# Two halves of one weight, side by side or apart: the order of weight pieces in an expert layer

## The reference

```
logits = t @ router_w                       # 256 tokens, 8 experts
top_v, top_i = top_k(logits, 2)
gates = softmax(top_v)
for e in range(8):
    out += combine[:, e] * ((silu(t @ w1[e]) * (t @ w3[e])) @ w2[e])
```

## Time and profile before

| | us |
|---|---|
| median of 3 runs | 2096.67 |
| lowest and highest run | 2094.08 and 2107.45 |
| the profiled execution's own time | 2105.79 |
| its span | 2104.0 |
| PE busy | 1988.3 (94%) |
| DVE busy | 1509.0 (72%) |
| ACT busy | 1087.0 (52%) |

### The profile page before, as it was taken

How to read it: one execution, slowest core, us unless ns; L and a number is a source line. 1 busy time by engine, 2 the same in 40 slices (tenths; PEclk the granted TensorE clock), 3 DMA queues, 4 the chain that set the end, 5 groups by cost and what they waited for, 6 DMA issues and landing times.

```text
span 2104.0 us, 25252 instructions
## 1 busy us (share of the span) xinstructions
PE 1988.3 (94%) x9922; PEld 1575.0 (75%) x9922; DVE 1509.0 (72%) x1829; ACT 1087.0 (52%) x1148; POOL 85.9 (4%) x78
## 2 busy tenths in 40 slices
PE   8989999999999899998999999999999999999997
PEld 7568588876587588786777777787777775759997
DVE  4666644447575698887789888898989886546666
ACT  1233234322241376775677766777777762535544
POOL 0130000000300000000100000000000000000000
PEclk9999999999999899999999999999999999899999
DMA  8200274343000499897799989999999983226450
GB/s 337 80 1 22 107 292 169 131 160 147 1 1 1 169 426 373 317 383 292 266 360 371 371 321 353 328 377 383 368 353 361 338 314 132 88 100 234 161 200 21
DMA packets 65152, 484.31 MB, mean 230 GB/s; under 512 B 9856, under 2 KB 12928, under 8 KB 13824
## 3 DMA queue, kind: packets, MB, share of 16 engines
q1 hardware_dynamic: 65024, 482.59, 60.6%
HBM read 481.51 MB, written 1.05 MB: 229 GB/s over the span
## 4 chain that ended last, share of the span: by engine, by line
PE 73%; DVE 14%; ACT 6%; issue 5%; DMA 1%; POOL 1%; SPq 0%; ACTq 0%; DVEq 0%; POOLq 0%
PE bank L741 13%; PE bank L1112 11%; PE bank L1114 10%; PE bank L1113 10%; PE bank L1117 7%; PE bank L1118 7%; DVE e_lo L2174 5%; PE bank L944 5%; ACT e_hi L2718 4%; PE bank L748 2%; DVE b_arena L1689 1%; PE bank L905 1%; PE bank L1374 1%; PE bank L1403 1%; DVE b_X L1695 1%
## 5 line engine op out<-in xcount | busy, mean ns | idle before, releaser
L2174 DVE TENSOR_TENSOR e_lo<-b_ring,e_hi 128x2048 fp32r<-128x2048 f32 (+1 forms) x407 | 916.7, 2279 | 208.9 <-ACT e_hi L2718 208.5
L2718 ACT ACTIVATE e_hi<-b_ring 128x2048 fp32r<-128x2048 f32 (+1 forms) x407 | 759.2, 1904 | 142.3 <-PE bank L1118 96.0
L1117 PE MATMUL bank<-e_hi,e_x 128*128 128x512 f32 x560 | 240.5, 429 | 16.2 <-DVE e_th L2178 14.2
L1118 PE MATMUL bank<-e_lo,e_x 128*128 128x512 f32 x560 | 223.1, 398 | 0.0
L1112 PE MATMUL bank<-e_hi,e_x 128*128 128x512 f32 (+1 forms) x416 | 161.4, 388 | 10.1 <-DVE e_lo L2174 7.0
L1114 PE MATMUL bank<-e_hi,e_x 128*128 128x512 f32 (+1 forms) x416 | 159.3, 383 | 0.0
L1113 PE MATMUL bank<-e_lo,e_x 128*128 128x512 f32 (+1 forms) x416 | 159.0, 382 | 0.0
L1117 PEld LDWEIGHTS bank<-e_hi,e_x 128*128 128x128 f32 x560 | 107.7, 192 | 50.2 <-DVE e_lo L2174 15.6
L1112 PE MATMUL bank<-e_hi,e_th 128*128 128x512 f32 x352 | 138.8, 394 | 1.2 <-DVE e_lo L2174 0.8
L1113 PE MATMUL bank<-e_lo,e_th 128*128 128x512 f32 x352 | 137.2, 390 | 0.0
L1114 PE MATMUL bank<-e_hi,e_tl 128*128 128x512 f32 x352 | 137.1, 389 | 0.0
(11 more groups left out here) (303 smaller groups left out, 3292.3 us busy)
## 6 DMA issues: line engine op xcount, KB each, us to landing
b_ring<-in_moe_w SPq DMA_DIRECT2D x336, 1024.0 KB, 7.0
b_ring<-in_ffn_w SPq DMA_DIRECT2D x15, 2048.0 KB, 8.0
b_ring<-in_w_in SPq DMA_DIRECT2D x14, 2048.0 KB, 8.4
b_ring<-in_w_up SPq DMA_DIRECT2D x12, 2048.0 KB, 8.0
b_ring<-in_w_down SPq DMA_DIRECT2D x6, 2048.0 KB, 7.8
b_ring<-in_w_o SPq DMA_DIRECT2D x4, 2048.0 KB, 8.0
b_gain<-in_gains SPq DMA_DIRECT2D x6, 1024.0 KB, 4.5
b_ring<-in_w_out SPq DMA_DIRECT2D x2, 2048.0 KB, 7.6
```

Of the source, the lines that this page charges most:

```text
L1117: e.matmul(out, both, bh, start=first, stop=False)
L1118: return e.matmul(out, both, bl, start=False, stop=last)
L2174: e.tensor_tensor(lo, raw, r32(hi), ALU.subtract).then_inc(lo_dve.sem)
L2718: return e.activation(out, x, ACT.Copy)
```

## The change

The largest expert's two halves of one weight (hf 0 and hf 1) get the same n. The formula's index i counts the 42 pieces; with `i - hf` the second half takes the place of the first one. Before, the places are 12, 16, 21, 25, 30, 35, ... up to 201, one piece behind every four or five small ones. After, they are 12, 21, 30, 39, 48, 58, 67, 76, 85, 94, 104, 113, 122, 131, 141, 150, 159, 168, 177, 187 and 196, two pieces behind every nine or ten small ones. The steps that hang on a second half move with it. Number and kind of all instructions, the small experts' order, the places of the other steps, the ring and the four pairs of split buffers stay.

```
@@ -275,7 +275,7 @@
     for i, (kind, u, hf) in enumerate(big):
-        n = 12 + 189 * i // 41
+        n = 12 + 189 * (i - hf) // 41
         put(n, "big", kind, u, hf)
         if hf == 1 and kind == "w1":
             put(n + 1, "big", "silu", u)
```

## The result

| | before | after |
|---|---|---|
| median, us (runs) | 2098.69 (4) | 2129.16 (4) |
| lowest and highest | 2094.08, 2107.45 | 2119.86, 2138.52 |
| profiled execution, its span | 2105.79, 2104.0 | 2119.86, 2118.1 |
| woven block in it | 765.1 | 793.0 |

What follows compares the result with a forecast made beforehand. PE bounds the block (busy 721.61 of 765.1 us), DVE close behind (655.58). 30 + 13 - 14 - 4 = +25, with clock +10 = +35: 2132 on the median, put at 2130; 8-in-10 range 2090 to 2150.

Steps and rivals of the forecast that it cites:

- Units with no big piece: At w3's first half of twelve units left without a big piece, PE stalls 2.5 us each: 30 us.
- rival B: In the woven block waits only move, long gathers letting DVE catch up: no change, +3 us, 2100; chance 0.17.
- step 3: DVE's down sums in units with pairs cost 8 us; other experts' gathers and finishes give 8 back: net 0.
- sign of being wrong: Prediction wrong in its core if units without a big piece pass without a PE wait of 2 us or more.
- Units with a pair: PE waits at w3's first half after a pair, 2.1 us to nothing by the pair's place: together 13 us.
- What goes away: PE's old waits vanish, 14.2 us for `e_th` and 4.0 for `b_pw`; the 7.1 for `e_h` stay.
- The clock: After long PE waits TensorE falls to 1.2 GHz, slowing a small piece by 1.6 us: +10, range nothing to 20.
- A: DVE's lead from a pair carries over, so waits for `e_th` and `b_pw` vanish: -18 us, 2079; chance 0.10.
- C: Transfers cannot keep up in all-small units, 1.8 us more in each of 12: +22 on top, 2152; chance 0.05.

## Why the prediction was right, step by step

The mechanism was right, and the forecast of 33 to 35 us lay close to the 30.5 measured. In part this was luck, since the terms below missed by more, in both directions.

1. **Units with no big piece: 30 us forecast, 24.4 measured.** In the profile after, w3's first half of the twelve units waited 0, 2.7, 2.1, 1.0, 2.5, 0, 2.7, 2.7, 0.4, 2.7, 5.0 and 2.5 us. Seven are at the forecast's 2.5 or within 0.4 of it. The four lowest, which fall 8.6 us short together, stand beside picks, gathers and finishes of other experts. That these keep PE busy while DVE catches up (rival B's argument, and the 8 us that step 3 had given back) is argued from their places; 5.0 is the unit with sum_in, one for one as step 3 has it. These four are also where the prediction's sign of being wrong, an empty unit that passes without a wait of 2 us, came up; eight of twelve had the wait. The run with all pairs ahead of the waiting point confirms the place: waits in empty units alone.

2. **Units with a pair: 13 us forecast, 11.3 measured, but not from where I said.** 9.9 of the 11.3 us stand in four of the seven down pairs' units, and half of that was the sums'. Without the sums all units with a pair wait 7.2 us, so this step was nearly twice too high. There the places behind w3's first half, down's second and down's first cost 3.0, 0.4 and 1.0 us, near the 2.1, 0.3 and 0.7 of the forecast; but pairs of w1 and w3 at the same places often cost nothing. The likely reason, their own folds and T, which lengthen PE's side, was not tested. That nothing is lost behind w1 held for all seven.

3. **Sums: net 0 forecast.** The gross price of 8 us agrees with the 7.6 us by which PE's waits fell in the run without the sums, of which 5.1 stood before `e_th` in the four units and 3.0 before `e_lo`. The gain against it, in step 1's low units, was about the size given. That this gain landed in step 1, and the sums in step 2, is why these two came out near their forecasts only in total.

4. **What goes away**: the 4.0 us for the sums' wait, gone; the 7.1 us for the multiplication, 7.6 after. Right. Not forecast: 3.9 us of PE's waits for `e_lo`, at small w1 pieces of four units behind down pairs.

5. **The clock: +10 forecast.** The wait of 4.99 us shows the fall: matmuls 0.43 us apart, TensorE at 1.2 GHz, until the piece's end.

```profile
1673.18 0.77 PE L1117 MATMUL bank<-e_hi,e_x 128*128 128x512 f32 x1 [4.99 <-DVE e_th L2178]
1673.74 0.63 PE L1118 MATMUL bank<-e_lo,e_x 128*128 128x512 f32 x1
1674.17 0.63 PE L1117 MATMUL bank<-e_hi,e_x 128*128 128x512 f32 x1
```

In the block of this execution 47 matmuls of the pieces started that far apart, against 33 before: 14 x 0.2 = 3 us. With the folds, turns and gathers, PE was busy 5.9 us longer there, as said above. By the clocks of whole executions it is the same size: the changed kernel's four have 0.982, 0.979, 0.978 and 0.974, the 17 runs of before beside the first four experiments a median of 0.982, and 0.982 - 0.9785 = 0.0035 of 2120 us is 7 us. So the split is about 22 us of waits and 6 or 7 of clock, near 30 in all; the forecast's 25 and 10 are both some 3 us too high. Of the nine waits of 2.47 us and more, six were followed by slow matmuls, within the "between half and all"; the wait of 2.72 us in unit 20 was not. But there were nine and not twelve, and two to six slow matmuls stood behind each, 0.4 to 1.2 us instead of 1.6. The clock also falls at places without such a wait: 23 of the 33 slow matmuls before. The clock term is read from these counts and busy times; no run took it away by itself.

Of the rivals, A fails: the waits grew, and the ratio's interval excludes it. The lead is not carried. ACT's place behind the fold, which I named as the reason, held in only half of the units tried. The other reason is argued: during a pair DVE stands still (24 us of new idleness before `e_lo`), since the four pairs of buffers let it work only three pieces ahead, and behind the pair it is busy without a gap, as in unit 20, and still late. B is right in its particular (gathers cover some units) and wrong in its sum. C fails: ACT nowhere waits for a landing.

**What stays open**: 17 to 21 us remain between pairs and singles when T's rest goes first, or both steps are moved. In the profiled executions the block is longer with pairs by 21.4 us (765.6 against 744.2) and 19.0 us (760.6 against 741.6). PE's waits, all added up, take 11.4 and 10.8 us of that, and PE is busy 9.7 and 7.9 us longer with the same matmuls. How much of this busy time is the clock, no run separates. A fifth pair of split buffers, which would show what the three pieces' limit is worth, was not tried, so whether pairs would cost anything with more buffers is open.

## What to carry to other kernels

When two engines are nearly level, what counts is not their totals over a stretch but what the slower one must have done by each waiting point: write down the steps queued ahead of the awaited one, and count how much of the faster engine's work stands in the same interval. Spread the long work so that every such interval has some; the same 21 pairs ran in 2117 or 2178 us by their places alone. And before moving work about, look at the awaited step's own place in its engine's queue: putting a step of 0.4 us ahead of one of 2.3 that nobody waited for yet gave back 28 us with pairs and 13 with singles, and combined with two more such moves it made the kernel 1.1% faster than it was.

## What the runs showed of the hardware

The spread between executions of one kernel, 13 us before and 19 after over four runs, goes with the mean granted clock, here of each execution's span: the changed kernel took 2118.1 us at 0.982, 2126.3 at 0.979, 2128.4 at 0.978 and 2136.7 at 0.974. A single profile of each kernel would have given half of the difference (14.1 us of 30.5). And waits of the same length, 2.7 us, were followed by the lower clock in some units and not in others: in the changed kernel in unit 29 but not in 6, 20 and 23, in the run with one more piece rounded before silu in 6 and 29 but not in 20. A wait of 2.10 us, in unit 9 of the changed kernel, was followed by it too, and matmuls started 0.43 us apart. Which ones fall is not set by the wait alone.
